# A skewed bias table of 16 rows per head instead of 128, and its rows loaded 16 queries at a time

## What is computed

```python
logits = einsum('bqgrd,bqkgd->bqgrk', q, k_sel) * A_HEAD_DIM ** -0.5
bias = rel_bias[rel_bucket(idx - qpos[None, :, None])]      # rel_bias is 32 buckets x 8 heads
p = softmax(where(valid, logits + bias, -inf))
```

## Time and profile before

| | |
|---|---|
| median of 3 runs | 1665.73 us (1665.21 to 1666.82) |
| profiled execution | 1664.78 us |
| its span from first to last instruction | 1662.4 us |
| TensorE busy | 1514.4 us, 91% of the span |
| VectorE, ScalarE, GpSimd busy | 690.3, 499.2 and 131.7 us |

### The profile page before, as it was taken

How to read it: one execution, slowest core, us unless ns; L and a number is a source line. 1 busy time by engine, 2 the same in 40 slices (tenths; PEclk the granted TensorE clock), 3 DMA queues, 4 the chain that set the end, 5 groups by cost and what they waited for, 6 DMA issues and landing times. The chain is left out here.

```text
span 1662.4 us, 29324 instructions
## 1 busy us (share of the span) xinstructions
PE 1514.4 (91%) x11818; PEld 1414.1 (85%) x11818; DVE 690.3 (42%) x1260; ACT 499.2 (30%) x852; POOL 131.7 (8%) x164
## 2 busy tenths in 40 slices
PE   5899999999999791998998889987999999999996
PEld 3799999999999791997896567687999999999996
DVE  2522332223323620588667556564422322233233
ACT  3532212211222420433324433532533112212233
POOL 2200000000001320000002031112100000000000
PEclk9999999999999895999899999999999999999998
DMA  8534434434324144312105021231222222222221
GB/s 304 176 122 148 143 115 145 145 114 141 101 66 132 46 85 56 95 51 64 51 14 147 2 62 30 69 90 58 60 80 70 70 77 76 76 64 76 69 70 64
DMA packets 205049, 150.64 MB, mean 91 GB/s; under 512 B 18139, under 2 KB 190460, under 8 KB 204952
## 3 DMA queue, kind: packets, MB, share of 16 engines
q1 hardware_dynamic: 191096, 99.79, 21.0%
q0 software_dynamic: 13856, 49.47, 9.7%
HBM read 139.99 MB, written 9.24 MB: 90 GB/s over the span
## 5 line engine op out<-in xcount | busy, mean ns | idle before, releaser
L2538 PE MATMUL pair<-h_hi,w_hi 128*128 128x320 f32 x1888 | 437.0, 313 | 3.7 <-ACTq L2292 2.3
L2538 PE MATMUL pair<-h_lo,w_hi 128*128 128x320 f32 x1888 | 432.4, 310 | 0.0
L2538 PE MATMUL pair<-h_hi,w_lo 128*128 128x320 f32 x1888 | 432.1, 310 | 0.0
L279 DVE TENSOR_TENSOR w_lo<-w_raw,w_hi 128x1024 fp32r<-128x1024 f32 x174 | 213.1, 1226 | 357.4 <-ACT w_hi L274 345.9
L2538 PEld LDWEIGHTS pair<-h_hi,w_hi 128*128 128x128 f32 x1888 | 316.1, 189 | 18.0 <-issue 14.0
L2538 PEld LDWEIGHTS pair<-h_lo,w_hi 128*128 128x128 f32 x1888 | 317.3, 189 | 0.1
L2538 PEld LDWEIGHTS pair<-h_hi,w_lo 128*128 128x128 f32 x1888 | 317.2, 188 | 0.1
L274 ACT ACTIVATE w_hi<-w_raw 128x1024 fp32r<-128x1024 f32 x174 | 182.9, 1054 | 338.2 <-PE pair L2538 177.3
L406 DVE SCALAR_TENSOR_TENSOR x_t<-pair,gate,x_t 128x320 f32 (+1 forms) x112 | 49.0, 479 | 212.4 <-PE pair L2538 153.1
L2538 PE MATMUL pair<-a_hi,w_hi 128*128 128x320 f32 x528 | 121.8, 312 | 2.2 <-DVEq L416 2.2
L2538 PE MATMUL pair<-a_hi,w_lo 128*128 128x320 f32 x528 | 120.3, 309 | 0.0
(11 more groups left out here) (369 smaller groups left out, 1634.9 us busy)
## 6 DMA issues: line engine op xcount, KB each, us to landing
w_mod_raw<-w_mod POOLq DMA_DIRECT2D x28, 1024.0 KB, 7.7
w_raw<-ffn_w_gate SPq DMA_DIRECT2D x44, 512.0 KB, 3.7
w_raw<-ffn_w_up SPq DMA_DIRECT2D x44, 512.0 KB, 3.8
w_raw<-ffn_w_down SPq DMA_DIRECT2D x32, 512.0 KB, 3.9
w_raw<-w_in SPq DMA_DIRECT2D x24, 512.0 KB, 3.8
w_raw<-ffn_w_down SPq DMA_DIRECT2D x16, 384.0 KB, 3.3
w_mod_a<-w_mod POOLq DMA_DIRECT2D x4, 1024.0 KB, 11.0
w_mod_b<-w_mod POOLq DMA_DIRECT2D x4, 1024.0 KB, 24.1
```

Of the source, the lines that this page charges most:

```text
L279: dve.tensor_tensor(w_lo[:, u % HL], w_raw[:, u % RAW], w_hi[:, u % HL].bitcast(F32), ALU.subtract).then_inc(lo_done, 1)
L2538: mm = pe.matmul(pair[u % 2][0:width, b, 0:HALF], w[:, 0:width], x_parts[part][:, k, b * HALF:(b + 1) * HALF], start=(k == 0 and v == 0), ...
```

## The change

The table in HBM holds 16 skewed rows per head (`SKEW`). Queries q0 to q0 + 15 read those 16 rows with a start that is q0 values further back. The eight loads of 128 queries for one head become 24 loads of 16 queries: eight for heads 0 and 2, eight for heads 1 and 3, and eight for heads 4 to 7. The four semaphores become three, and jobs 2 and 3 wait for the same one.

```diff
+SKEW = 16
-        skewed = nc.dram_tensor("bias_rows", (AH, P * (REL + 1)), F32, kind="Internal").ap()
+        skewed = nc.dram_tensor("bias_rows", (AH, SKEW * (REL + 1)), F32, kind="Internal").ap()
...
-            for k in range(4):
-                for s in range(2):
-                    h = head_of(k, s)
-                    sp.dma_start(rel8[:, h], bass.AP(skewed.tensor, skewed.offset + h * P * (REL + 1) + P - 1, [[REL, P], [1, SEQ]]))\
-                        .then_inc(S[f"rel_in{k}"], 16)
+            for n_, (h0, h1, step) in enumerate(((0, 4, 2), (1, 4, 2), (4, 8, 1))):
+                for q0 in range(0, P, SKEW):
+                    rows = bass.AP(skewed.tensor, skewed.offset + h0 * SKEW * (REL + 1) + P - 1 - q0,
+                                   [[REL, SKEW], [step * SKEW * (REL + 1), (h1 - h0 + step - 1) // step], [1, SEQ]])
+                    sp.dma_start(rel8[q0:q0 + SKEW, h0:h1:step], rows).then_inc(S[f"rel_in{n_}"], 16)
...
-            pool.dma_start(bass.AP(skewed.tensor, skewed.offset, [[P * (REL + 1), AH], [REL + 1, P], [1, REL]]),
-                           tbl[0:AH].unsqueeze(1).broadcast_to([AH, P, REL])).then_inc(S["tbl_out"], 16)
+            pool.dma_start(bass.AP(skewed.tensor, skewed.offset, [[SKEW * (REL + 1), AH], [REL + 1, SKEW], [1, REL]]),
+                           tbl[0:AH].unsqueeze(1).broadcast_to([AH, SKEW, REL])).then_inc(S["tbl_out"], 16)
...
-                                                             [[P * (REL + 1), AH], [REL, TB], [1, n]])).then_inc(S["rel_s"], 16)
+                                                             [[SKEW * (REL + 1), AH], [REL, TB], [1, n]])).then_inc(S["rel_s"], 16)
...
-                    dve.wait_ge(S[f"rel_in{j}"], 32)
+                    dve.wait_ge(S[f"rel_in{min(j, 2)}"], 16 * P // SKEW)
```

More of the change, by code:

```diff
@@ L505, in encoder_step @@
                    "nv std_o on ot_mm o_gate prepared kvs so so_out s_in mix_hi mix_lo st_out "
-                   "rel_in0 rel_in1 rel_in2 rel_in3 rel_s logits nmax exp prob pt_mm pt pv att "
+                   "rel_in0 rel_in1 rel_in2 rel_s logits nmax exp prob pt_mm pt pv att "
                    "k_in0 k_in1 v_in0 v_in1 kb_turned kb qz chain achain raw_extra").split():
```

## The result

The change makes the kernel faster: 1622.36 us median of 4 runs (1621.36 to 1627.85) against 1665.47 us before, a ratio of 0.9754 with a 95% interval of 0.9723 to 0.9786. That is 43.1 us between the medians. Forecast were 38.6 us and 1627.1 us, with a range from 1625.0 to 1631.0.

A forecast was written before the change was run, and what follows sets the result against it. TensorE, busy 91% of the span, bounds the kernel, with one long hole, a 36.8 us wait near 626 us. Hole 39.1 us less bias loads 0.5 gives 38.6 us gained: 1627.1 us, range 1625.0 to 1631.0.

The forecast's parts named there:

- The write: Table write into `bias_rows`, issued at 605.63 us: 16 rows per head instead of 128, landing in 7 to 10 us, not 55.3.
- How late it may be: The write may take until 624.0 us, 18.4 us after its issue, before TensorE waits; 8 us to spare.
- What the hole costs: TensorE's stop from 625.96 to 662.90 us: 36.9 us idle plus 2.2 us at half clock, 39.1 us.
- rival C: Write doesn't shorten with its rows, or the load was late for another reason: 1666 or about 1640 us; chance 0.05.
- The chain across the hole: Write, `w_in` load behind it, ScalarE's `split_hi`, copy out of PSUM, TensorE's transposes; removing the stall removes it whole.
- The bias loads: Before job 0: eight issues for heads 0 and 2 make VectorE wait 0.5 us, range 0 to about 5 us.
- rule on 16 partitions: Transfers to 16 partitions run at some 104 GB/s: heads 0 and 2 take 5.0 us, a stall of a few tenths.
- The sets for the later jobs: Heads 1 and 3 land by 904.5 us, needed at 907.65; heads 4 to 7 by 911.9, needed at 917.24.
- the `s_in` loads: Queued behind the bias loads on SyncE: 10.8 us later, landing by 923 us, first reader at 956.2; no cost.
- The sum and the range: 39.1 - 0.5 = 38.6 us off 1664.78, plus 0.95 for the median: 1627.1 us, range 1625.0 to 1631.0.
- B: At job 0, bias loads of heads 0 and 2 come 2 to 6 us late: 1629 to 1633 us; chance 0.12.
- D: New 16-partition loads run on one or two DMA engines each, job 0 waits 82 us: 1710 us; chance 0.02.

The follow-up runs named there:

- skew64: The changed kernel with `SKEW = 64`, 64 rows per head and 6 loads of 64 queries; median 1636.77 us, ratio 0.9832.
- eight_loads: The changed kernel with 8 bias loads in place of 24, each 16 queries of all eight heads; median 1633.27 us, ratio 0.9821.
- The two clean shifts: The changed kernel with 8 or 16 unread identity products on TensorE ahead of the first `tm` transposes; medians 1628.85 and 1626.07 us.
- copy_before_split: The kernel before, with ScalarE's copy of a `tm` unit out of PSUM put ahead of the split; median 1657.10 us, ratio 0.9954.
- delay10: The changed kernel with ten repeated, unread one-hot products on TensorE ahead of the second half of the table; median 1637.53 us.

## Why the prediction was wrong in its number and right in its mechanism

*The write.* Forecast 7 to 10 us, measured 8.2. The slope per row is 0.42 us where 0.43 was taken, over four sizes.

*How late it may be.* Forecast 18.4 us, 17.7 by skew64, where the first load landed 1.0 us after the write and not 0.2. The changed write uses less than half of it.

*What the hole costs.* Forecast 39.1 us, of which 2.2 at half clock; measured 39.3 at the third `tm` transposes. That it is given back nowhere held too: the same distance stands between the copies to `small` (680.89 and 641.63).

*The rule that was set aside.* Under rival C the prediction quotes the Trainium skill ("DMA: Bandwidth & Descriptors", "Queues, rings and completion order"): an engine changes between its queues at every packet. It concludes that by this rule the loads would have been done well before the write, and that the trace does not agree. That reading was wrong. The packets of the hole, 97 of the write and 96 of the loads in 10 us, agree with the rule. The prediction left out that one turn of the write takes an engine some 0.81 us, so that the 64 turns of a load last about as long as the whole write. It cost the forecast nothing, because it went by the landing times.

*The chain across the hole.* Shown: with the write alone restored the hole is back (36.8 us), and with ScalarE's order reversed it moves one unit on and shrinks to 31.2 us.

*The bias loads.* This is the first term that was off: 0.5 us of waiting were forecast and none was there. The issues were 0.53 us apart, between the two pitches weighed, and the early loads landed in 2.0 to 2.5 us. The sets for the later jobs and the `s_in` loads were hidden, as forecast. The Trainium skill's rule on 16 partitions ("Door 1: The DMA port swizzle", as above), which the prediction left open, roughly agrees with the trace: 114 GB/s as 8 loads beside its 104.

*The sum and the range.* This is the step that failed. It took a time and a spread from three runs, "half a microsecond for the runs", and carried TensorE's clock behind the hole over unchanged, which puts that term at nothing. The runs showed two things in its place. Executions of either kernel have a standard deviation of 2.5 us, and it goes with the clock: over 88 executions of the kernel before, the shortest have a span of 1657.5 us at a mean granted clock of 0.967 and 0.968 and the longest 1669.4 us at 0.959. And in the mean 1.7 us more than the terms of the sum were gained. The 4.7 us between 1627.1 and 1622.36 add up like this, rounding apart: 0.7 from starting at 1665.73, where the mean of the kernel before is 1665.02; 0.2 at the hole; 0.5 at the bias loads; 1.7 that the means have gained beyond that; and 1.7 by which the median of these four runs lies under the changed kernel's own mean of 1624.06. That last term is the luck of four executions. But the mean is still 0.9 us below the range, so luck alone does not account for the miss.

*The rivals.* B, C and D did not happen. A late start of job 0, as in B, did come in eight_loads, at 11.4 us, when one set held all heads. D supposed that the small loads take 4.9 us or more each, one after the other; the first nine, issued some 0.5 us apart, landed in 2.0 to 2.5 us.

*What stays open* are the 1.7 us (0.4 to 2.9) that the changed kernel gains in the mean beyond the hole. In the traces they go with the stretch at the first sample rows: with the full hole all five traces have it, and the changed kernel has it in two of four. Whether the change makes it rarer by moving the work in time, as placement says, or by taking the full hole away, is not shown. The two clean shifts departed by +1.6 and -1.4 us with an error of 1.2, and copy_before_split shows in one trace that a hole can be there without it.

## What to carry to other kernels

Look for the transfer whose landing coincides with another's: a large, slow write from few partitions can hold up a small load that shares its engines, since here each packet of the load waited for a much longer packet of the write. And an in-order engine that waits for such a load also holds back the copies queued behind the wait. Work out how late the transfer may be, since below that its size costs nothing and above it every microsecond counts, plus the restart at half clock. Before giving a range, ask how far single executions of the same kernel lie apart, and compare traces of equal clock before explaining a few microseconds.

## What the runs showed of the hardware beyond the forecast

- The write from 8 partitions took 8.2, 14.9, 28.4 and 55.3 us for 16, 32, 64 and 128 rows of 2560 bytes per head: 8 x 2560 bytes every 0.42 us, 49 GB/s. During it the engines' busy share was 0.49. Two 512 KB loads issued 1 and 2 us behind it took 9.0 and 9.4, 15.5 and 15.9, 28.6 and 28.9, and 54.6 and 55.0 us, where such a load otherwise takes 3.8. During the write of 128 rows the engines served one packet of the loads (512 bytes) for each packet of the write (5 KB, 0.81 us of an engine), 96 and 97 in 10 us.
- 2.10 MB into 128 partitions by transfers of 16 partitions ran at 114 GB/s, by transfers of 128 partitions at 184 GB/s, both beside some 0.8 MB of stores.
- TensorE's clock fell to the 1.2 GHz level (0.51 over 609 to 616 us) while TensorE was busy throughout, behind products with 32 x 8 weights (delay10). It isn't only standing still that brings it down.
- The same program had the half-clock stretch at its first sample rows in two traces of four; the input stage was 3.6 to 4.7 us longer in these. A kernel with a hole of 31 us ran the same rows at full clock (copy_before_split).
